# Sixteen gate units as rounded products inside a recurrence, and a merge stage that starts with the attention branch

## What is computed

```python
h = rmsnorm(x, norm1_g); p = h @ w_in
p_rwkv, q, k, v, gate_logits = split(p)
y_a = rwkv7_bidirectional(p_rwkv, ...) @ w_o_rwkv     # 8 heads, both directions, group norm, gate g
y_b = neighbourhood_attention_2d(q, k, v, ...) @ w_o_na
g_a, g_b = split(sigmoid(gate_logits + b_gate))       # 1024 columns each
x = x + (g_a * y_a + g_b * y_b) @ w_out
x = x + hierarchical_moe(rmsnorm(x, norm2_g), ...)
```

## Time and profile before

| | us |
|---|---|
| median of 3 runs (lowest, highest) | 1964.38 (1963.19, 1971.38) |
| span of the profiled execution | 1966.5 |
| TensorE busy | 1823.0 (93%) |
| VectorE busy | 1017.0 (52%) |
| ScalarE, GpSimd busy | 632.7 (32%), 322.0 (16%) |
| mean granted clock of TensorE | 0.966 |

### The profile page before, as it was taken

The page is one execution under the profiler, slowest core; times in us unless marked ns, Lnnn a source line. Parts: engine busy times, 40 slices in busy tenths (PEclk is TensorE's granted clock), DMA queues, the critical chain, the costliest instruction groups (busy, mean ns, idle before and its releaser), DMA issues. The chain is left out here.

```text
span 1966.5 us, 44872 instructions
## 1 busy us (share of the span) xinstructions
PE 1823.0 (93%) x19153; PEld 1349.5 (69%) x19153; DVE 1017.0 (52%) x1844; ACT 632.7 (32%) x1208; POOL 322.0 (16%) x489
## 2 busy tenths in 40 slices
PE   7999989999999978998889999899998999999998
PEld 5777667777757753333357877677777787888887
DVE  7666544444468971111147775566667574333334
ACT  5555434334133221211133643012222253313321
POOL 1000144243222321111100000002322001001100
PEclk9999999999999978999979999999999999999999
DMA  6222110000057879999983211620001334333331
GB/s 219 80 78 75 43 34 14 15 24 14 14 200 262 289 265 361 409 409 410 404 328 111 65 54 53 214 75 25 24 3 68 113 103 139 97 97 90 96 104 43
DMA packets 76827, 271.59 MB, mean 138 GB/s; under 512 B 11494, under 2 KB 13926, under 8 KB 75360
## 3 DMA queue, kind: packets, MB, share of 16 engines
q1 hardware_dynamic: 62528, 230.25, 33.0%
q10 hardware_dynamic: 8640, 27.00, 3.9%
q0 software_dynamic: 5472, 11.59, 1.6%
HBM read 257.09 MB, written 19.40 MB: 141 GB/s over the span
## 5 line engine op out<-in xcount | busy, mean ns | idle before, releaser
L216 DVE TENSOR_TENSOR weights_lo<-ring,weights_hi 128x1024 fp32r<-128x1024 f32 (+1 forms) x134 | 161.9, 1210 | 148.4 <-ACT weights_hi L212 148.4
L212 ACT CAST weights_hi<-ring 128x1024 fp32r<-128x1024 f32 (+1 forms) x134 | 137.1, 1025 | 223.7 <-PE ps L242 219.3
L241 PE MATMUL ps<-wide_b_round,weights_hi 128*128 128x512 f32 (+1 forms) x368 | 136.7, 371 | 0.0
L240 PE MATMUL ps<-mlp_hi,weights_hi 128*128 128x512 f32 (+1 forms) x327 | 121.4, 371 | 1.1 <-DVE weights_lo L216 1.1
L241 PE MATMUL ps<-mlp_lo,weights_hi 128*128 128x512 f32 (+1 forms) x327 | 120.5, 368 | 0.0
L242 PE MATMUL ps<-mlp_hi,weights_lo 128*128 128x512 f32 (+1 forms) x327 | 120.4, 368 | 0.0
L240 PE MATMUL ps<-wide_a_round,weights_hi 128*128 128x512 f32 x216 | 92.3, 427 | 0.0
L240 PE MATMUL ps<-h_tail,weights_hi 128*128 128x512 f32 x232 | 91.6, 395 | 0.7 <-DVE weights_lo L216 0.6
L1072 PE MATMUL ps<-wide_a,ring 128*128 128x256 f32 x320 | 91.3, 412 | 0.0
L242 PE MATMUL ps<-h_tail,weights_lo 128*128 128x512 f32 x232 | 90.9, 392 | 0.0
L241 PE MATMUL ps<-h_tail_rest_round,weights_hi 128*128 128x512 f32 x232 | 90.4, 390 | 0.0
(11 more groups left out here) (646 smaller groups left out, 4119.0 us busy)
## 6 DMA issues: line engine op xcount, KB each, us to landing
ring<-stream_in SPq DMA_DIRECT2D x207, 512.0 KB, 3.7
moe_ring<-stream_in SPq DMA_DIRECT2D x112, 512.0 KB, 14.3
w_mod<-w_mod_in ACTq DMA_DIRECT2D x40, 512.0 KB, 5.9
wide_b<-stream_in SPq DMA_DIRECT2D x32, 512.0 KB, 12.5
xT<-w_mod_in SPq DMA_DIRECT2D x16, 512.0 KB, 4.6
na_rel<-rel_in POOLq DMA_DIRECT2D x4, 640.0 KB, 4.4
mod_acc<-mod_part ACTq DMA_DIRECT2D x5, 512.0 KB, 8.2
ring<-mod_acc SPq DMA_DIRECT2D x1, 2560.0 KB, 19.7
```

The costliest lines, as they stand in the source:

```text
L212: act.copy(self.hi[:, i % self.n, at:], w[:, at:]).then_inc(self.cast.sem, self.cast.up())
L216: ins = eng.tensor_tensor(self.lo[:, i % self.n, at:], self.unit(i)[0][:, at:], self.hi[:, i % self.n, at:], ALU.subtract)
L240: pe.matmul(out, left[0], right[0], start=start, stop=False, **kw)
L241: pe.matmul(out, left[0], right[1], start=False, stop=False, **kw)
```

## The change

**Gates.** All 16 gate units are computed in the recurrence, as rounded products from the two parts of `h`: `STEPS` = 24 steps of 128x512 a unit, 384 steps: 72, 48, six times 36, 24, 24. The joins go. ScalarE rounds each unit's weights into the storage of `ybT`, GpSimd subtracts in the ring slot itself, at level 4 of a round (`GATE_MID`) or at its end (`GATE_END`, rounds 0, 1, 3, 5, 7). ScalarE writes a gate to one of two buffers, and SyncE stores gates 0 to 13 in device memory; the last two stay. The attention output is stored in device memory by GpSimd's queue in the head stage, and comes back late in the recurrence, where ScalarE and GpSimd split it. In the last two rounds VectorE forms mean and variance of three of the four token chunks, and GpSimd scales `v` and adds `lnx_b`.

**Merge.** The stage loads the parked gates (1.5 MB first, on SyncE's queue, ahead of the net's input; 2 MB later) and starts with the `g_up` product. A unit of branch outputs now belongs to one branch and is used in two halves: eight half units of attention first, with the norm beside them, then the transposes and eight half units of the recurrence's branch, each 12 rounded products into one of three banks. VectorE weighs each half by its gate. GpSimd adds the two branches (`mix`) and makes the remainder (`mix_rest`), and it subtracts the weights of units 1 to 3 and 10 to 15. The mod sums share a `w_mod` load between two sums (24 loads instead of 40); 2 sums stand beside the attention halves, 10 beside the others, 28 beside the output product. The residual and the window are loaded later, the DFT matrix earlier. Elsewhere only the name of a constant changes.

```diff
+                for p in range(4):
+                    pool.wait_ge(y_copied.sem, y_copied.at(p + 1))
+                    pool.dma_start(k.dram["yb_parked"][:, p, :], yT[:, p, :]).then_inc(y_saved.sem, y_saved.up(16))
+                pool.wait_ge(y_saved.sem, y_saved.at(64))
...
-EARLY, STEPS = 10, 16
...
+GATES, STEPS, LAST_STEPS = 16, 24, 16
+KEPT = GATES - 2
...
+GATE_MID = {0: ((0,), (2,)), 1: ((2,), (4,)), 2: ((4,), (6,)), 3: ((), (7,)), 4: ((7,), (9,)), 5: ((), (10,)), 6: ((10,), (12,)),
+            7: ((), (13,)), 8: ((13,), (15,))}
+GATE_END = {0: ((1,), (3,)), 1: ((3,), (5,)), 2: ((5,), ()), 3: ((6,), (8,)), 4: ((8,), ()), 5: ((9,), (11,)), 6: ((11,), ()),
+            7: ((12,), (14,)), 8: ((14,), ())}
+GATE_STEPS = [72, 120, 156, 192, 228, 264, 300, 336, 360, 384]
...
-                            landed, full = k.take()[1:]
-                            pe.wait_ge(landed, full)
+                            k.take()
+                            pe.wait_ge(w_rested.sem, w_rested.at(u + 1))
...
-                        if u == 0 and at == 0:
-                            pe.wait_ge(h_joined.sem, h_joined.at(kt + 1))
-                        w = k.ring[:, (k.taken_at_stage + u) % RING, kt * P:(kt + 1) * P]
-                        mm = pe.matmul(k.ps[:, 2 + u % 2, at:at + 256], w, k.A[:, kt, at:at + 256],
-                                       start=s == 0, stop=s + 2 >= STEPS, skip_group_check=True)
+                        mm = pe.matmul(k.ps[:, 2 + u % 2, :], w_lo[:, slot(u), ws] if part == 2 else w_hi[:, u % 2, ws], h[part % 2][:, kt, :],
+                                       start=s == 0, stop=s + 1 == STEPS, skip_group_check=True)
...
                         if j:
-                            gates(3)
+                            gates(7 if i < 2 else 6)
...
                 def scores(i, b):
                     if i == 0:
-                        gates(3 if b else 2)
+                        gates(7 if b else 5)
                     elif b:
-                        gates(2)
+                        gates(5)
...
                     if i + 1 == N:
-                        keep_busy(k, pe, 4, 4)
+                        gates(6)
...
-                    if i + 1 == N:
-                        gates(1)
-                        keep_busy(k, pe, 1, 4)
-                    else:
-                        gates(2)
+                    gates(4)
...
                     if i + 1 == N:
-                        keep_busy(k, pe, 4, 6)
+                        gates(2)
+                        keep_busy(k, pe, 3, 4)
                     else:
-                        gates(2)
+                        gates(5)
...
-                    gates(2 if t else 3)
+                    gates(5 if t else 7)
...
-                            gates(1)
+                            gates(2 if t < 2 else 1)
...
+                                    gates(6)
+                    gates_done(t)
+                assert step == GATES * STEPS, step
...
+                def leave_gate(i):
+                    act.wait_ge(k.used, k.after(i))
+                    if i >= 2:
+                        act.wait_ge(gate_saved[i % 2].sem, gate_saved[i % 2].at(16 * (i // 2)))
+                    act.activation(out[:, i % 2, :], k.ps[:, 2 + i % 2, :], ACT.Sigmoid, bias=k.col("b_gate", i)).then_inc(
+                        gate_left.sem, gate_left.up())
+                def round_weights(u):
+                    act.wait_ge(k.landed[slot(u)], k.full(k.taken_at_stage + u))
+                    if u >= 2:
+                        act.wait_ge(k.used, k.after(u - 2))
+                    act.copy(w_hi[:, u % 2, :], k.ring[:, slot(u), :]).then_inc(w_rounded.sem, w_rounded.up())
+                def serve(at, t):
+                    leave, ahead = at.get(t, ((), ()))
+                    for i in leave:
+                        leave_gate(i)
+                    for u in ahead:
+                        round_weights(u)
...
-                def join(b):
-                    dve.tensor_tensor(k.A[:, b, :], h[0][:, b, :], h[1][:, b, :], ALU.add).then_inc(h_joined.sem, h_joined.up())
+                def norm_sums(c, n, step):
...
+                        dve.wait_ge(y_done.sem, y_done.last)
+                        ins = dve.tensor_reduce(mean, yh, AX.X, ALU.add)
+                    if step == 1:
+                        ins = dve.tensor_scalar(mean, mean, 1.0 / HD, None, ALU.mult)
+                    if step == 2:
+                        ins = dve.tensor_tensor(yh, yh, mean.unsqueeze(2).broadcast_to([P, n * RH, HD]), ALU.subtract)
+                    if step == 3:
+                        dve.wait_ge(t_ready.sem, t_ready.at(2 * N))
+                        dve.wait_ge(s_ready.sem, s_ready.at(4 * N))
+                        ins = dve.tensor_tensor(sq, yh, yh, ALU.mult)
+                    if step == 4:
+                        ins = dve.tensor_reduce(var, sq, AX.X, ALU.add)
...
+                def rest_weights(u):
+                    pool.wait_ge(w_rounded.sem, w_rounded.at(u + 1))
+                    pool.tensor_tensor(w_lo[:, slot(u), :], k.ring[:, slot(u), :], w_hi[:, u % 2, :], ALU.subtract).then_inc(
+                        w_rested.sem, w_rested.up())
+                    pool.wait_ge(w_rested.sem, w_rested.last)
...
+                        if lv == 4:
+                            for u in GATE_MID.get(t, ((), ()))[1]:
+                                rest_weights(u)
...
+                    pool.wait_ge(yb_rounded.sem, yb_rounded.at(b + 1))
+                    pool.tensor_tensor(yb_lo[:, b, :], yb_in[:, b, :], yb_hi[:, b, :], ALU.subtract).then_inc(yb_rested.sem, yb_rested.up())
...
+                for i in range(GATES):
+                    k.stream(sp, i + 1)
+                    if i < KEPT:
+                        sp.wait_ge(gate_left.sem, gate_left.at(i + 1))
+                        sp.dma_start(k.dram["gates_parked"][:, i, :], out[:, i % 2, :]).then_inc(gate_saved[i % 2].sem, gate_saved[i % 2].up(16))
...
-                for i in range(LATE):
...
-                    for kt in range(DB):
-                        mm = pe.matmul(k.ps[:, gate_bank(i), :], wg[:, kt * P:(kt + 1) * P], k.A[:, kt, :], start=kt == 0, stop=kt == DB - 1)
...
+                def half(n, first):
...
+                    if n >= 3:
+                        pe.wait_ge(h_done.sem, h_done.at(n - 2))
+                    for kt in range(4):
+                        if n == 8:
+                            pe.wait_ge(ya_rested.sem, ya_rested.at(kt + 1))
+                        mm = product(pe, k.ps[:, half_bank(n), :], w.parts(i, (4 * e + kt) * P, (4 * e + kt + 1) * P), y_parts(first + kt), kt == 0, kt == 3)
...
+                for t in range(NT):
+                    mm = pe.matmul(k.ps[:, 4 + t, :], lora[:, 2, t * P:(t + 1) * P], g_up, start=True, stop=True)
+                mm.then_inc(u_ready.sem, u_ready.up())
+                layer(0)
+                for n in range(8):
+                    half(n, 4)
+                    if n == 5:
...
+                    if n == 4:
+                        layer(1)
+                for n in range(8, 16):
+                    half(n, 0)
...
+                for i in range(3):
+                    w.round(act, i)
+                act.wait_ge(var_done.sem, var_done.at(1))
+                act.activation(stat[:, 1, :], stat[:, 1, :], ACT.Sqrt, scale=1.0 / HD, bias=GN_EPS).then_inc(rooted.sem, rooted.up())
+                net_copy(0)
+                w.round(act, 3)
+                w.round(act, 4)
+                net_sin(0)
+                net_copy(1)
+                w.round(act, 5)
...
+                def weigh(n):
...
+                    x = gate((n + 8) % 16)
+                    if n == 0:
+                        dve.wait_ge(g_in.sem, g_in.at(16))
+                    if n == 8:
+                        dve.wait_ge(b_in.sem, b_in.at(16))
+                    dve.tensor_tensor(x, x, k.ps[:, half_bank(n), :], ALU.mult).then_inc(h_done.sem, h_done.up())
...
+                w.rest(dve, 0)
+                first_sums()
+                group_norm(0)
+                weigh(0)
+                group_norm(1)
+                weigh(1)
+                group_norm(2)
+                weigh(2)
+                group_norm(3)
+                weigh(3)
+                dve.wait_ge(k.used, k.after(3))
+                w.rest(dve, 4)
+                weigh(4)
+                weigh(5)
+                for b in range(RB):
+                    y_rest(b)
+                weigh(6)
+                mod_steps(6)
+                w.rest(dve, 5)
+                weigh(7)
+                mod_steps(7)
...
                 for i in range(8):
...
+                    if i % 2 == 0:
+                        w.rest(dve, 6 + i // 2)
+                    weigh(8 + i)
+                    mod_steps(8 + i)
...
-                    if 10 + i < 16:
-                        w.rest(dve, 10 + i)
...
+                def mix(i):
```

(29 more changed lines are left out.)

451 lines of the change are left out of this document (212 added, 239 removed).

## The result

| | before | after |
|---|---|---|
| median of four runs each (lowest, highest), us | 1966.8 (1963.2, 1971.4) | 1988.3 (1987.9, 1990.3) |
| span of the profiled execution, us | 1966.5 | 1986.1 |
| TensorE, VectorE busy, us | 1823.0, 1017.0 | 1814.6, 1015.8 |
| GpSimd busy, us | 322.0 | 430.0 |
| mean granted clock of TensorE | 0.966 | 0.955 |

The ratio is 1.011, with a 95% interval of 1.0097 to 1.0123. The forecast was 1968.3, its range 1948 to 1984. TensorE has 8 us less to do in all and the kernel takes 20 more, so the time is in waits and in the clock.

A forecast was written before the change was run, and what follows sets the result against it. TensorE was taken to bound the recurrence and the merge's first two stretches, VectorE the third. Terms 20.2 - 9.1 - 15.0 + 1.0 + 6.8 = +3.9 on 1964.4 gave 1968.3 us, range 1948 to 1984.

The forecast's parts named there:

- The recurrence, +20.2: Recurrence: gate steps +20.4, fillers -2.2, first round -1.3, held state scaling +2.7, later keys +0.6; from +10 to +28 us.
- 2.7 + 0.6: Recurrence: GpSimd's subtractions hold VectorE's state scaling, +2.7 us; a rounding and subtraction ahead of the first keys, +0.6.
- steps, fillers and the first round: Recurrence: more gate steps +20.4 us, fewer idle fillers -2.2, first round's extra steps falling into a wait -1.3.
- So I take all of it: Recurrence: all added gate time lengthens it, none absorbed by idle time; low bound, half of 26 idle us absorb it, -10.
- First stretch, -9.1: Start of the merge: 40.9 us against 50.0, as six f32 gate units go and waits for net input and sine come.
- Second half units, -15.0 and +1.0: Merge's second stretch: 28.8 us against 43.8, paced by VectorE and GpSimd excluding each other; output product waits 1.0 more.
- Third stretch, +6.8: Output product, residual and logits: VectorE's changed sums and remainders -3.7 us, GpSimd's subtractions +10.5; from -3.7 to +10.
- five subtractions of 2.1, which hold VectorE up: +10.5: Third stretch: GpSimd's five weight subtractions, 2.1 us each, hold VectorE up beside the folds, +10.5 us.
- Rival 1: Half units, third stretch and state scaling: GpSimd's short operations fit under weighings and waits; 1951.8 us, chance 0.30.
- The 9.07: Trace before: four modulation sums took 9.07 us on VectorE beside GpSimd's work, where one alone takes 1.28.
- Rival 2: Second half units: GpSimd finishes last with 17 operations, output product starts 8.4 us later; 1976.7 us, chance 0.18.
- rival 3: Recurrence: products wait for prepared weights at the head of four rounds, 2 us each, +8; 1976 us, chance 0.10.

The follow-up runs named there:

- small-subtractions run: Changed kernel with GpSimd's sixteen recurrence weight subtractions on 64 of 1024 columns and rounded weights in each block's third product: 1975.0 us, ratio 1.0069.
- two-products run: Changed kernel with 112 of the recurrence's 384 gate products (rounded input by the weights' remainder) left out: 1976.3 us, ratio 1.0064.
- first experiment: Changed kernel with the gate net's input and small weights loaded ahead of the parked gates on SyncE's queue: 1982.7 us, ratio 1.0115.
- the small sums: Changed kernel with VectorE's ten modulation sums beside GpSimd's adds made on 64 of 1024 columns: 1974.8 us, ratio 1.0076.
- the products on ScalarE: Changed kernel where ScalarE multiplies the weights of ten modulation sums into PSUM and VectorE adds them from there: 1977.9 us, ratio 1.0058.
- the fourth buffer: Changed kernel with a fourth buffer for the partial modulation sums, so VectorE need not wait for the first row's store: 1980.6 us, ratio 1.0068.
- The two edits to VectorE's queue: Two separate runs on the changed kernel: five late weight subtractions moved from GpSimd to VectorE, 1979.0 us; one more buffer for partial sums, 1980.6 us.
- the kernel with three more edits: Changed kernel with modulation sums on TensorE (128x2 products), recurrence and late subtractions on VectorE, and net's input loaded first: 2006.2 us, ratio 1.0193.
- the fourth kernel: Changed kernel with modulation sums on TensorE (weights moving), recurrence and late subtractions on VectorE, and net's input loaded first: 1989.8 us, ratio 1.0116.
- the first kernel: Changed kernel with the modulation sums moved from VectorE to TensorE as eight 128x2 products a chunk, nothing else changed: 2013.5 us, ratio 1.0230.

## Why the prediction was wrong

**The recurrence, +20.2.** The sum of its work was right by luck, for its parts were not: 21.6 measured, but the small-subtractions run puts GpSimd's subtractions at 9 us and not at 2.7 + 0.6 (the held state scaling was found, 0.67 twice; where the rest of the 9 lies is not shown, the keys that I gave "as much slack" among the candidates), which leaves 12 for steps, fillers and the first round, where I had 16.9. The two-products run fits: 17 to 21 of 26 us of gate products are on the path, and I took all. The rest is the clock. The step that failed is "So I take all of it": that step weighed whether microseconds find idle time and priced them all at one clock, while the stays at half clock took 6.5 us more than before on average and 10.3 more in this profile, nearly the whole 11.0 by which the line missed. The prediction added 1.7 for a stop in the merge and nothing for the recurrence, whose stretch passed the "over 28" that was to prove it wrong (31.2, and 28.1 on average). Work alone would not have passed it.

**First stretch, -9.1 (measured -8.1).** Right within a microsecond, though two terms were small: the wait for the net's input took 8.9 for 7, and the half clock cost 2.5 for 1.7 (of the 5.1 lost from 587 to 598, 2.6 fell in the wait itself). The wait for the sine took 0.3 for 1.7. That the first experiment got back 2 us of a wait of 9 shows that the norm's root and the argument chain stood close behind.

**Second half units, -15.0 and +1.0 (-12.9).** That the two engines hold each other up is shown by the small sums and by the products on ScalarE. The rows below "what would show it" answered: VectorE's sums read 1.7 where 2 was expected, and GpSimd's adds 2.26. Waits for weighings came once, at the end: TensorE ran through all eight half units at its own pace and then stood still 9.0 us.

**Third stretch, +6.8 (+14.2).** The mis-sized term is "five subtractions of 2.1, which hold VectorE up: +10.5". Moving them gave 7.3 us net of 6.1 that VectorE then spends on them itself, so they cost 13.4, 2.9 more than the term. Two waits of VectorE had no term at all. One is for the first row's way to device memory, 4.9 us, of which the fourth buffer gave back 2.7; the other is for the first output block, 5.8 us, with nothing else in VectorE's program ahead of that residual add (before, it waited 0.4). VectorE's waits in the third stretch of after:

```profile
DVE xT L1996 <- PE ps L242: 6.6, 2, 5.8
DVE mod_part L1937 <- DMA mod_acc<-mod_part: 4.9, 1, 4.9
```

What the second costs by itself no run shows. The clock is not the cause here, though the clock lost rose from 5.7 to 13.9: in six profiles in which this stretch is unchanged it took 85.7 to 85.9 us, with 10.5 to 13.9 lost. The one of "the net's input first" has the least:

```profile
647.20:733.10 85.90, 65.65 (x288) 49.90 (x289) 65.96 (x45) 16.84 (x23) 48.02 (x23) 0.88 0.52 165
```

The two edits to VectorE's queue did shorten it, to 78.6 and 83.2. So that queue sets this stretch, as the prediction said. The residual adds are 9.7 us apart on average (8.0 before), "as before or wider".

**The rivals.** Rival 1 (the door costs little) fell: GpSimd's adds took 2.26, not 1.3. The 9.07 had stood against it, and it was rightly given less. Rival 2 is what happened in its stretch and was already most of the -15.0; as a separate +8.4 it counted the same delays twice. Of rival 3's waits for prepared weights after has one, of 0.9 us, not 8 in all. The chance for slower, 0.28, had no case in it that ended above 1985: it had no term for the clock in the recurrence, so the range was too short on that side. How far is partly chance: run again on another chip, the same kernel took 1983.8.

That the changed recurrence loses 17.3 us to the clock and the old one 10.8 is shown on nine and three profiles; what in it tips a given stop into a fall is not shown and stays open.

## What to carry to other kernels

When work is moved into gaps, give the clock a term of its own: list the stops that are already there, and price a fall (here up to 1.7 us for each stay of 3.4) for those that are not followed by one yet. Then ask which engine sets the pace of the stretch: in the recurrence the falls lengthened it, in the third stretch they did not. Where VectorE streams two SBUF operands beside GpSimd, count on each holding the other up (here adds of 1.29 became 2.26); if ScalarE is idle, let it put one operand into PSUM, and here that was gone with the sums unchanged. And count an f32 product by products, not by records.

## What the runs showed of the hardware

TensorE can be busy by its records and slow: with 128x2 products it was busy 111.4 of 112.7 us at a mean granted clock of 0.76 (and in the kernel with three more edits it lost 28.5 of 114.6 us in this stretch). With the same weights moving past two columns (128x512 products) it stayed at 1.00 over 89 us, busy 86.7, and again in the fourth kernel. The narrow products alone do not do it: in the second stretch, where a single chunk of them stood between twelve 128x512 products at a time, the first kernel lost nothing in 36.4 us; in the third, two or three chunks stood together. Fewer gate products, other things equal, meant more clock lost (32.4 against 17.3 us), so taking 26.1 us of them out made the recurrence 6.2 us shorter.
